# A front woven from weight tiles and small stages, and a new order of GpSimd's and VectorE's work in the recurrent stage

## The reference

```python
h = rmsnorm(x, norm_mix)
sb_q, sb_k, sb_v, sb_g, gla_q, gla_k, gla_v, gla_r, gla_g, sgu_u, sgu_v, sgu_g = split(h @ w_in)
o_sb  = stick_breaking_attention(sb_q, sb_k, sb_v)        # 8 heads of 128
o_gla = gla_chunked(gla_q, gla_k, gla_v, log_sigmoid(gla_r @ w_gate_up + b) / 16)  # 4 heads
o_sgu = chunked_sgu(gelu(sgu_u), gelu(sgu_v), sgu_norm, w_sgu, b_sgu)
mix = rmsnorm(concat(o_sb, o_gla, o_sgu) by head) * silu(concat(sb_g, gla_g, sgu_g))
x = x + mix @ w_out
x = x + cross_attention(rmsnorm(x), rmsnorm(mem), w_xq, w_xkv, w_xo)     # 4 heads, 256 memory rows
x = rmsnorm(x, final_norm)
```

```python
S_t = S_{t-1} diag(decay_t) + (S_{t-1} a_t) b_t^T + v_t k_t^T ;  y_t = S_t r_t
```

## Time and profile before

| | |
|---|---|
| median of the runs | 3768.68 us (3 runs, 3767.18 to 3769.16) |
| profiled execution | 3771.53 us, its span 3769.8 us |
| granted TensorE clock, mean | 0.942 |
| PE busy | 3398.0 us, 90% |
| DVE busy | 2248.3 us, 60% |
| ACT busy | 1573.3 us, 42% |
| POOL busy | 403.7 us, 11% |

### The profile page before, as it was taken

The page is one execution under the profiler, slowest core; times in us unless marked ns, Lnnn a source line. Parts: engine busy times, 40 slices in busy tenths (PEclk is TensorE's granted clock), DMA queues, the critical chain, the costliest instruction groups (busy, mean ns, idle before and its releaser), DMA issues.

```text
span 3769.8 us, 60030 instructions
## 1 busy us (share of the span) xinstructions
PE 3398.0 (90%) x19704; PEld 2946.3 (78%) x19704; DVE 2248.3 (60%) x3082; ACT 1573.3 (42%) x2146; POOL 403.7 (11%) x573
## 2 busy tenths in 40 slices
PE   5999575868995988899899999998999999999997
PEld 5888464756884877888788888887877788888886
DVE  5555466636667455545666565666555575656565
ACT  3333432334556545453434343433344343434342
POOL 1000100300002332323000000030000300000002
PEclk8999786988998999999999999998999999999999
DMA  4667131524773000005566666665643656666664
GB/s 125 189 179 189 36 90 34 158 76 125 208 210 101 18 26 18 26 10 156 155 188 183 186 185 184 186 185 139 180 123 100 178 156 189 188 188 187 184 187 125
DMA packets 1000230, 523.13 MB, mean 139 GB/s; under 512 B 25590, under 2 KB 996236, under 8 KB 999372
## 3 DMA queue, kind: packets, MB, share of 16 engines
q1 hardware_dynamic: 994944, 508.88, 47.8%
q0 software_dynamic: 4464, 12.85, 1.0%
q10 hardware_dynamic: 732, 0.22, 0.0%
HBM read 513.50 MB, written 8.39 MB: 138 GB/s over the span
## 4 chain that ended last, share of the span: by engine, by line
PE 83%; DVE 9%; ACT 4%; issue 3%; POOL 1%; DMA 0%; DVEq 0%; ACTq 0%; POOLq 0%
PE proj L289 46%; PE proj L291 23%; PE side L1718 1%; PE side L1743 1%; DVE g L439 1%; PE side L417 1%; PE side L1614 1%; DVE a_scratch L1101 1%; PE side L1757 1%; PE side L970 1%; PE side L1598 1%; DVE w_low L245 1%; PE side L631 0%; PE side L630 0%; PE side L1600 0%
## 5 line engine op out<-in xcount | busy, mean ns | idle before, releaser
L261 DVE TENSOR_TENSOR w_low<-w_raw,w_high 128x1024 fp32r<-128x1024 f32 x904 | 1117.8, 1237 | 839.5 <-ACT w_high L258 836.7
L289 PE MATMUL proj<-a_pair,w_high 128*128 128x512 f32 x3808 | 1356.2, 401 | 64.5 <-DVE a_pair L434 30.2
L258 ACT ACTIVATE w_high<-w_raw 128x1024 fp32r<-128x1024 f32 x900 | 952.9, 1059 | 1087.1 <-PE proj L291 1085.0
L289 PE MATMUL proj<-b_pair,w_high 128*128 128x512 f32 x3776 | 1342.6, 400 | 52.6 <-DVE g L299 16.5
L291 PE MATMUL proj<-a_pair,w_low 128*128 128x256 f32 x3808 | 1075.8, 283 | 0.0
L291 PE MATMUL proj<-b_pair,w_low 128*128 128x256 f32 x3776 | 1066.7, 282 | 0.0
L289 PEld LDWEIGHTS proj<-a_pair,w_high 128*128 128x128 f32 x3808 | 722.0, 190 | 246.0 <-issue 59.9
L289 PEld LDWEIGHTS proj<-b_pair,w_high 128*128 128x128 f32 x3776 | 716.4, 190 | 228.0 <-issue 28.8
L291 PEld LDWEIGHTS proj<-a_pair,w_low 128*128 128x128 f32 x3808 | 728.4, 191 | 0.0
L291 PEld LDWEIGHTS proj<-b_pair,w_low 128*128 128x128 f32 x3776 | 723.0, 191 | 0.1
L299 DVE TENSOR_REDUCE g<-proj 128x256 f32<-128x512 f32 (+1 forms) x277 | 189.2, 683 | 0.0
(11 more groups left out here) (468 smaller groups left out, 2975.8 us busy)
## 6 DMA issues: line engine op xcount, KB each, us to landing
w_raw<-in_mlp_w_up_dram SPq DMA_DIRECT2D x256, 512.0 KB, 4.1
w_raw<-in_mlp_w_down_dram SPq DMA_DIRECT2D x256, 512.0 KB, 3.9
w_raw<-in_w_in_dram SPq DMA_DIRECT2D x112, 512.0 KB, 3.8
w_raw<-in_rwkv_w_rkv_dram SPq DMA_DIRECT2D x96, 512.0 KB, 4.2
w_raw<-in_w_kvf_dram SPq DMA_DIRECT2D x64, 512.0 KB, 4.1
w_raw<-in_w_out_dram SPq DMA_DIRECT2D x32, 512.0 KB, 4.0
w_raw<-in_rwkv_w_o_dram SPq DMA_DIRECT2D x32, 512.0 KB, 4.0
w_raw<-in_fox_w_q_dram SPq DMA_DIRECT2D x32, 512.0 KB, 3.9
```

Source lines behind the costliest of these rows:

```text
L258: eng.activation(wh[slot][:], raw[slot][:], ACT.Copy).then_inc(sem("w_hi"), 1)
L261: eng.tensor_tensor(wl[slot][:], raw[slot][:], wh[slot][:].bitcast(F32), ALU.subtract)\
L289: pe.matmul(ps[bank][:, :].rearrange("p (a n) -> p a n", a=2), wh[slot][:, k, :], pair[:, :, kk, :], start=kk == 0, stop=False)
```

## The change

The front is woven. `phases` names the projections by kind; the first 57 tiles form a list FRONT and are written out one by one (`single`), and between them stand the small stages, each engine's part at its place. Tile numbers n count from 0.

- Start: x is loaded first, by halves of tokens. Its squares are summed by two ScalarE activations with accumulation (no matmuls), the sums become a row by `token_row`, and TensorE turns x into the transposed layout. The same for the memory, behind tile 0 on ScalarE, without a stop between tiles 1 and 2.
- Tiles 0 to 23 (`in_q`) are the query, key and value tiles of stick-breaking; its heads go in pairs at n = 6, 8, 10 and so on to n = 28 (`sb_scores`, `sb_sums`, `sb_result`). Then come the tiles of the gated recurrence (24 to 32), of the gating unit (33 to 40) and of the gates (41 to 56). The norm of the first eight heads is made at n = 30 to 32; the gated recurrence begins at n = 33, its nine levels stand at n = 35 to 43, its result at 45; the norm of its four heads is at 49; the gating unit's work ends at 52, and the norm of the last four heads is at 54. Four gates (`gates(0)` to `gates(3)`, each a sigmoid on ScalarE with GpSimd's and VectorE's products for four heads) follow as their tiles are done, on ScalarE and VectorE between the splits; the last one stands behind the front, so that `out` waits for it with its last four blocks of rows.
- `out` with its 16 tiles follows the front. The memory's keys and values (`xk`, `xv`, four tiles each) now stand behind `out`, on both sides of `xq`; the norm of x for cross attention is made between the `xk` tiles, the heads' scores behind the `xq` tiles, and their results behind the `xv` tiles.
- Recurrent stage, GpSimd: floor before the mask RK and the load of v; in `decayed` the product av first, then bt, then kt; the four products of r leave GpSimd; reset of T before the load of the next pair.
- Recurrent stage, VectorE: takes the four products of r (`read`) at the end of a pair; `weighted` from behind the last level to level 2; `bonus` from level 5 to behind it.

The diff, cut to its core:

```diff
-    ("in_a", 40, False), ("in_r", 1, False), ("in_b", 16, False), ("xkv", 8, False),
-    ("out", 16, False), ("xq", 4, False), ("xo", 4, True),
+    ("in_q", 24, False), ("in_l", 8, False), ("in_r", 1, False), ("in_u", 8, False), ("in_g", 8, False), ("in_h", 4, False),
+    ("in_s", 4, False), ("out", 16, False), ("xk", 4, False), ("xq", 4, False), ("xv", 4, False), ("xo", 4, True),
...
+        def heads_src(t, j):
+            return cols(win, (t % 3) * 1024 + (t // 3) * P)(0, j)
...
+            for u in range(8):
+                pe.wait_ge(sem("x_in"), 32)
+                if u == 7:
+                    pe.wait_ge(sem("tr_d"), 1)
+                for x in range(4):
+                    k, b = 2 * u + x // 2, x % 2
+                    mm = pe.transpose(xbank[u][:, P * x:P * x + P], xtok[:, b, P * k:P * k + P], ident[:])
+                mm.then_inc(sem("tr"), 1)
...
+            def token_row(event, ready):
+                pe.wait_ge(*after(ready))
+                for b in range(2):
+                    mm = pe.matmul(q[1][:, P * b:P * b + P], rstd[:, 0, P * b:P * b + P], ident[:], start=True, stop=True)
+                mm.then_inc(*once(event))
...
+            def mix_sums(g, heads, bank, src):
+                pe.wait_ge(sem("mx_sq"), g)
+                for i in range(heads):
+                    mm = pe.matmul(q[bank][0:heads, 0:S], wsel[:, 7 - i:7 - i + heads], src(i), start=i == 0, stop=i == heads - 1)
+                mm.then_inc(sem("mx_sum"), 1)
...
+            for n, (name, t) in enumerate(FRONT):
+                single(name, t, project(pe, name, BHL, ("x_done", lambda g: g + 1) if n == 0 else None))
+                p, step = divmod(n, 6)
...
+                if step == 0 and 1 <= p <= 4:
+                    sb_scores(p - 1)
+                if step == 2 and 1 <= p <= 4:
+                    sb_sums(p - 1)
+                if step == 4 and 1 <= p <= 4:
+                    sb_result(p - 1)
+                if n == 30:
+                    mix_sums(1, 8, 5, lambda i: G[:, 8 + i, :])
+                if n == 32:
+                    mix_rows(1, 8, (0, 1, 2, 3))
+                if n == 33:
+                    gla_begin()
+                if 35 <= n <= 43:
+                    gla_level(n - 34)
+                if n == 45:
+                    gla_result()
...
+                if n == 49:
+                    mix_rows(2, 4, (4, 5))
+                if n == 50:
...
+                if n == 54:
+                    mix_rows(3, 4, (1, 2))
+            for t in range(16):
+                single("out", t, project(pe, "out", AHL, ("mix_done", lambda g: g + 1) if t == 0 else None))
...
+            for b in range(2):
+                act.wait_ge(sem("x_in"), 32)
+                act.activation(flat_of(BF, 8 * b, 8), xtok[:, b, :], ACT.Square, accum_out=tokstat[:, b:b + 1]).then_inc(sem("tok_sq"), 1)
+            act.wait_ge(sem("tok_sq"), 2)
+            act.activation(tokstat[:, 4:6], tokstat[:, 0:2], ACT.Sqrt, scale=1.0 / D, bias=eps[:, 0:1]).then_inc(*once("std_x"))
...
+                if n == 0:
+                    for b in range(2):
+                        act.wait_ge(sem("mem_in"), 32)
+                        act.activation(flat_of(AF, 0, 8), mtok[:, b, :], ACT.Square, accum_out=tokstat[:, 2 + b:3 + b]).then_inc(sem("tok_sq"), 1)
+                        act.wait_ge(sem("tok_sq"), 3 + b)
+                    act.activation(tokstat[:, 6:8], tokstat[:, 2:4], ACT.Sqrt, scale=1.0 / D, bias=eps[:, 0:1]).then_inc(*once("std_m"))
...
+            gates(3)
+            high(3)
...
+                if n == 48:
+                    dve.wait_ge(*after("sg_std"))
+                    dve.wait_ge(sem("mx_row"), 6)
+                    ch.after(dve.reciprocal(rstd[:, 1, :], rstd[:, 0, :]))
+                    for g in range(4):
+                        o = dve.scalar_tensor_tensor(out=G[:, 48 + g, :], in0=G[:, 48 + g, :], scalar=col("sgu_norm", g),
+                                                     in1=rstd[:, 1, :], op0=ALU.mult, op1=ALU.mult)
+                    o.then_inc(*once("sg_v"))
+                    low(0)
...
+                if n == 49:
+                    gelu(1, 0)
+                    mix_norm(2, 4, (4, 5), 32, 8, 4)
...
+            gates(0)
...
+            gates(1)
+            gates(2)
+            gates(3)
...
+            for t in range(4):
+                single("xk", t, project(pe, "xk", BHL, ("mem_done", lambda g: g + 1) if t == 0 else None))
+                if t == 0:
+                    norm_tensor(pe, "xattn")
+            for t in range(4):
+                single("xq", t, project(pe, "xq", AHL, norm_ready("xattn") if t == 0 else None))
+                if t:
+                    scores(t - 1)
+            for t in range(4):
+                single("xv", t, project(pe, "xv", BHL))
+                if t == 0:
+                    scores(3)
+                elif t == 1:
+                    turned(0)
...
-            st = Steps(pool, "rw_rt")
...
-                        pool.wait_ge(sem("rw_rt"), 2 * pv(j - 1, s))
+                        pool.wait_ge(sem("rw_rt"), pv(j - 1, s))
...
             def decayed(j):
                 for s in range(2):
                     t, d = RW_T[s], RW_S[s]
+                    pool.wait_ge(sem("rw_kk"), pv(j, s))
+                    pool.tensor_tensor(t["av"], t["kk"], t["av"], ALU.mult).then_inc(sem("rw_ab"), 1)
+                for s in range(2):
+                    t, d = RW_T[s], RW_S[s]
+                    pool.wait_ge(sem("rw_ab"), pv(j, s))
                     pool.wait_ge(sem("rw_exp"), pv(j, s))
+                    pool.tensor_tensor(d["bt"], t["av"], t["ex"], ALU.mult).then_inc(sem("rw_bt"), 1)
+                for s in range(2):
+                    t, d = RW_T[s], RW_S[s]
                     pool.wait_ge(sem("rw_k1"), pv(j, s))
                     pool.tensor_tensor(d["kt"], t["in"][:, 1, :], t["ex"], ALU.mult).then_inc(sem("rw_kt"), 1)
-                for s in range(2):
-                    t, d = RW_T[s], RW_S[s]
-                    for h in range(2):
-                        k = st.do(pool.tensor_tensor(d["rt"][j % 2][rng(h), h, :], t["in"][rng(h), 0, :], t["cm"][rng(h), :], ALU.mult))
-                        st.need(k)
-                    pool.wait_ge(sem("rw_kk"), pv(j, s))
-                    pool.tensor_tensor(t["av"], t["kk"], t["av"], ALU.mult).then_inc(sem("rw_ab"), 1)
-                for s in range(2):
-                    t, d = RW_T[s], RW_S[s]
-                    pool.wait_ge(sem("rw_ab"), pv(j, s))
...
                     keys(j)
                 mask(i, "RB", ALU.is_ge)
+                if i < LAST:
+                    floor(j)
                 mask(i, "RK", ALU.is_ge)
                 if i < LAST:
                     load_values(j)
-                    floor(j)
                     decayed(j)
+                    reset_t(j)
                     if j < LAST:
                         load(j + 1)
-                    reset_t(j)
...
+            def read(j):
+                for s in range(2):
+                    t, d = RW_T[s], RW_S[s]
+                    for h in range(2):
+                        o = dve.tensor_tensor(d["rt"][j % 2][rng(h), h, :], t["in"][rng(h), 0, :], t["cm"][rng(h), :], ALU.mult)
+                    o.then_inc(sem("rw_rt"), 1)
...
+            read(0)
...
+                    elif lv == 2 and i < LAST:
+                        weighted(j)
                     elif lv == 3 and i < LAST:
                         removed(j, ka)
                     elif lv == 4 and i:
                         kf = scaled(fin, kf)
-                    elif lv == 5:
-                        if i:
-                            gated(fin, kf)
-                        if i < LAST:
-                            bonus(j)
+                    elif lv == 5 and i:
+                        gated(fin, kf)
...
-                        weighted(j)
                         decayed(j)
                 if i < LAST:
+                    bonus(j)
...
+                if i < LAST:
+                    read(j)
...
```

1239 lines of the change are left out of this document (709 added, 530 removed).

## The result

The changed kernel takes 3570.74 us, the median of four runs from 3567.6 to 3582.7, against 3768.0 for the kernel before on the same chip: a ratio of 0.9482, 95% interval 0.9459 to 0.9505. The forecast was 3576, with a range of 3530 to 3635. Busy shares are now PE 93%, DVE 62%, ACT 44%, POOL 11%, the mean granted clock 0.967 instead of 0.942.

A forecast was written before the change was run, and what follows sets the result against it. TensorE was taken to wait through serial small stages in the front and at two places in the recurrent stage. Gains 34 + 103 + 18 + 38 = 193 off 3771.5, less 2.8 for the median, give 3576 us; range 3530 to 3635.

The forecast's parts named there:

- Start: Before tile 2: x loaded first, squares on ScalarE, memory norm behind tile 0; tile 2 at 43.2 instead of 77.2, gain 34.0.
- Chores: Small stages between and behind the front's tiles: cost falls from 204.8 to 102 us, gain 103.
- stalls: Front: TensorE waits at the first level, tiles 51 and 52 and the fourth gate, together 20.2 us.
- changeovers: Front: stepping in and out of a tile, 0.2 us each, about 5 over the 35 steps with a chore.
- Norm of x and cross attention: Norm of x and cross attention beyond its tiles: cost falls from 42.4 to 24.5 us, gain 18.
- Recurrent stage: Pairs of chunks: masked-copy wait 2.0, last-copy wait 1.7, half speed 1.8; five and a half for seven pairs, gain 38.
- VectorE as the bound: Front: chores in VectorE's in-order queue cost some 40 steps 1.4 us more each, 56, giving 3632; chance 0.17.
- The recurrent stage without a gain: Next pair's load waits for the moved reads, puts a wait before every pair and eats the 38: 3614; chance 0.12.
- The weight supply: Chores hold VectorE's splits so late that weight loads stop overlapping in 85 woven tiles: 332 us, 3908; chance 0.02.

The follow-up runs named there:

- the run with added work: Changed kernel with one more VectorE pass of 1.23 us in each of tiles 2 to 56 of the front; 3583.2 us, ratio 0.9504.
- the recurrent order alone: Kernel before the change, with only the new order of the recurrent stage; 3726.7 us, ratio 0.9878.

## Why the prediction was right, point by point

*Start.* First projection forecast at 26, tile 2 at 43.2; they came at 24.7 and 42.1. Transfer (8.9 in place of 9) and squares (3.9 in place of 4.3) were sized a little too long, as was what follows them.

*Chores.* Forecast 102 for what is left, measured 102.4, and made up of other shares. Of the 496.4 us TensorE spends 71.9 on its own small products (forecast 69, and 1.8 of it is the first level at half speed), 16.5 in stalls (20.2), 4 to 6 in projections at half speed (8), and what is left, 8 to 10, in changeovers (5). The stalls came at the places named and nowhere else: 4.80 at the first level (forecast 6.7), 0.91 and 3.37 behind tiles 50 and 51 (1.3 and 4.8), 7.40 at the fourth gate (7.4). GpSimd's full-width product took 2.34 (2.7). The changeovers were undersized: an error of three to five that the stalls and the clock made good. That the sum meets the forecast to half a microsecond is luck also in another way. Seven other kernels run the same 71 tiles with the same waits to within 1.3 us, and theirs took 498.1 to 508.0 us, which by the same subtraction leaves 104 to 114; the profiled execution of the changed kernel was the shortest of the eight.

*Norm of x and cross attention.* 25.4 against 24.5, but turned about inside: the norm's last group costs waits of 0.5, 1.0 and 5.0 where I had 3, and the last head 4.0 where I had 9.

*Recurrent stage.* 44.5 instead of 38; a pair went from 61.4 to 54.2 on average, idle time from 6.8 to 2.8 and busy time from 54.7 to 51.4. The joint part's wait went whole (3.7 and 1.5 in turn, 2.6 a pair, forecast 1.7). That leaves 1.4 for the wait at the masked copy, forecast 2.0, with ScalarE late next as named (1.35 in the place of 3.0). The clock gave 3.2, forecast 1.8. So two terms were too small and one too large: 7.2 a pair where I had 5.5. I had multiplied by seven; six pairs gave 43.4 of the 44.5. I had taken as clock only what one row showed at half speed and not the shorter stretches behind other waits. Undone by itself the floor costs 20.0 and the two products 17.6. The other 6.9 show only with all of the old order back; no run undid just those two, so that they are an interaction is argued. The moved r products and GpSimd's new order, undone alone, cost the stage nothing (456.6 and 458.1 against 460.4).

*Elsewhere* I had nothing, and 6 us were lost between the end of cross attention and the end, with the same waits as before and a clock of 0.92 instead of 0.93 in the first of the two stretches. That is within what these parts vary by from one execution to the next (below). The profiled sum is 5 above the forecast because +6.5, +4 and +1 stand against -6 and -1.

*The rivals.* VectorE as the bound: refuted by the run with added work. The recurrent stage without a gain: refuted; the distance of 2.0 us in front of the masked copy behind the next load was forecast, 2.20 is what the timeline shows, and it never became a wait of TensorE. VectorE does wait for the later load now, 16 us in all over seven pairs, but has the time. The Trainium skill says ("SBUF — State Buffer", "SBUF: two separate sides") that GpSimd's DMAs cannot write descriptors while VectorE holds the shared ports. No row here isolates that, and it made no difference that shows: the two issues took 0.76 and 0.73 and landed in 3.0 to 3.9 us, before in 3.1 to 4.3. The weight supply: no wait of TensorE for it stands among those of the front.

What stays open is which waits let the clock fall, and what makes the spread from 3567.6 to 3582.7. Two things vary between the profiled executions. From tile 2 to the end of cross attention, kernels with the same front and nearly the same waits have between 17 and 48 matmul pairs that follow each other at 0.64 instead of 0.35 us, 5 to 14 us in sum; the profiled execution of the changed kernel was one of the two best. And the stretch behind the recurrent stage, where all the kernels are alike, took between 2054.2 and 2065.5 us at the same granted clock of 0.98 (the r products back, and GpSimd's old order):

```profile
1506.41:3560.60 2054.19, 1975.47 (x11100) 1706.61 (x11098) 1273.98 (x1705) 819.32 (x934) 153.57 (x164) 0.98 0.59 171
```

```profile
1512.72:3578.20 2065.48, 1987.20 (x11100) 1709.58 (x11098) 1276.03 (x1705) 819.46 (x934) 151.85 (x164) 0.98 0.59 170
```

TensorE's waits there sum to 71 us in both; its matmuls take longer, and no run shows why. So the clock is not all of it: among the changed kernel's own four runs the one with the highest mean clock, 0.967, is not the shortest. No run separates the two shares.

## What to carry to other kernels

Walk each engine's queue to the places where it holds the engine that sets the pace, and price those few; the average share of an engine says nothing about them. Where a stall is removed, name the engine that is late next and move that too: a copy put ahead of five exponentials took one more microsecond out of each pair. Count with each removed wait the half speed that can come behind it. In the recurrent stage it was 3.2 us a pair beside 4.0 of idle time, and where one cause was put back it was up to three and a half times the added wait; behind the last wait of 1.35, in most pairs, it was nothing.

## What the runs showed of the hardware that I had not expected

The price of a short wait depends on what other waits stand near it, and not on that alone. A wait of 1.35 us for ScalarE's copy was followed by full speed in five of the six pairs of the changed kernel (53.9 us a pair) and in four of six with the recurrent order alone; in the others it was followed by a stretch of half speed (55.5). With the wait at 0.3 or less, none of the twelve pairs of two kernels fell. Where 0.9 us of other waiting was added, the first pair took 54.8 us at full clock, the next 56.5, and each of the last four 58.1 at a clock of 0.94: there 0.9 us of waiting cost 4.1 us of time. Pairs with the same work and the same waits came out at either level, so what decides it is not shown.
